# A two-block transformer kernel on one core: own work lists for the last delta rounds, and the stick-breaking softplus of later key blocks added on VectorE

## The reference, cut to what matters

```python
# stick-breaking attention, one head: z[q, k] = q . k / sqrt(128)
visible = key_pos < q_pos
log_keep = where(visible, log_sigmoid(-z), 0)          # -softplus(z)
log_w = log_sigmoid(z) + cumsum_from_the_right(log_keep, keys) - log_keep
o = where(visible, exp(log_w), 0) @ v

# delta rule, one head, chunks in sequence; v is silu(conv(...)) too
u, w = solve(I + lower, [v * beta, k * beta * exp(g)])
v_new = u - w @ S
o = q_dec @ S + attn @ v_new
S = S * g_last + k_dec.T @ v_new
```

## Time and profile before

| | us |
|---|---|
| median of three runs | 2892.74 |
| profiled execution | 2892.34 |
| its span | 2890.1 |
| TensorE busy | 2813.6 (97%) |
| VectorE busy | 1480.2 (51%) |
| ScalarE busy | 1141.9 (40%) |
| GpSimd busy | 513.5 (18%) |
| start of delta round 6 (first fill of unit 41) | 1942.50 |
| first product of the stick stage | 2096.03 |
| first weights product of head 0 | 2133.54 |

### The profile page before, as it was taken

How to read it: one execution, slowest core, us unless ns; L and a number is a source line. 1 busy time by engine, 2 the same in 40 slices (tenths; PEclk the granted TensorE clock), 3 DMA queues, 4 the chain that set the end, 5 groups by cost and what they waited for, 6 DMA issues and landing times.

```text
span 2890.1 us, 37115 instructions
## 1 busy us (share of the span) xinstructions
PE 2813.6 (97%) x14501; PEld 2248.5 (78%) x14501; DVE 1480.2 (51%) x2064; ACT 1141.9 (40%) x1699; POOL 513.5 (18%) x297
## 2 busy tenths in 40 slices
PE   8999999999999999998999999999989999999999
PEld 4888888856656688887888888887867777788887
DVE  6634434266547533336755565554256665653443
ACT  4211212224444422224655555553376553432221
POOL 0000000023111000003434443434322223100000
PEclk9999999999999999999999999999999999999999
DMA  6522323143103233323211121211211113322332
GB/s 233 157 75 89 105 77 103 51 153 97 37 30 142 85 92 92 95 94 103 71 48 49 52 66 54 65 45 45 68 56 52 59 44 104 97 96 94 95 95 80
DMA packets 69872, 241.77 MB, mean 84 GB/s; under 512 B 8219, under 2 KB 8347, under 8 KB 69315
## 3 DMA queue, kind: packets, MB, share of 16 engines
q1 hardware_dynamic: 62032, 221.28, 23.9%
q10 hardware_dynamic: 7666, 18.13, 1.9%
HBM read 232.74 MB, written 6.64 MB: 83 GB/s over the span
## 4 chain that ended last, share of the span: by engine, by line
PE 87%; ACT 6%; DVE 5%; issue 1%; DMA 1%; ACTq 0%; DVEq 0%; POOL 0%; SPq 0%; POOLq 0%
PE ps L1076 61%; PE ps L1460 3%; PE ps L1266 2%; PE ps L1554 2%; PE ps L1235 2%; PE ps L1357 2%; PE ps L1397 2%; PE ps L1253 1%; PE ps L1287 1%; PE ps L1389 1%; ACT w_hi L447 1%; PE ps L1106 1%; PE ps L1531 1%; ACT r L447 1%; DVE f_t L465 1%
## 5 line engine op out<-in xcount | busy, mean ns | idle before, releaser
L1076 PE MATMUL ps<-Nh,w_hi 128*128 128x512 f32 (+1 forms) x1808 | 661.6, 366 | 14.3 <-DVE Nl L454 6.2
L1076 PE MATMUL ps<-Nl,w_hi 128*128 128x512 f32 (+1 forms) x1808 | 630.7, 349 | 0.0
L1076 PE MATMUL ps<-Nh,w_lo 128*128 128x512 f32 (+1 forms) x1808 | 628.4, 348 | 0.0
L447 ACT ACTIVATE w_hi<-w_raw 128x1024 fp32r<-128x1024 f32 (+1 forms) x352 | 368.1, 1046 | 638.4 <-PE ps L1076 524.2
L454 POOL TENSOR_TENSOR w_lo<-w_raw,w_hi 128x1024 fp32r<-128x1024 f32 x125 | 307.7, 2462 | 780.2 <-ACT w_hi L447 776.4
L454 DVE TENSOR_TENSOR w_lo<-w_raw,w_hi 128x1024 fp32r<-128x1024 f32 (+1 forms) x227 | 281.8, 1242 | 257.4 <-ACT w_hi L447 247.3
L1076 PEld LDWEIGHTS ps<-Nh,w_hi 128*128 128x128 f32 x1808 | 343.2, 190 | 85.4 <-issue 35.4
L1076 PEld LDWEIGHTS ps<-Nl,w_hi 128*128 128x128 f32 x1808 | 343.4, 190 | 50.8 <-issue 6.0
L1076 PEld LDWEIGHTS ps<-Nh,w_lo 128*128 128x128 f32 x1808 | 343.2, 190 | 44.0
L1076 PE MATMUL ps<-x1h,w_hi 128*128 128x512 f32 (+1 forms) x784 | 272.3, 347 | 3.3 <-DVE x1l L465 1.9
L1076 PE MATMUL ps<-x1l,w_hi 128*128 128x512 f32 (+1 forms) x784 | 266.6, 340 | 0.0
(11 more groups left out here) (345 smaller groups left out, 4749.5 us busy)
## 6 DMA issues: line engine op xcount, KB each, us to landing
w_raw<-in_w_in SPq DMA_DIRECT2D x132, 512.0 KB, 3.5
w_raw<-in_w_proj SPq DMA_DIRECT2D x89, 512.0 KB, 3.5
w_raw<-in_w_ada SPq DMA_DIRECT2D x52, 512.0 KB, 4.3
w_raw<-in_w_out SPq DMA_DIRECT2D x48, 448.0 KB, 3.3
w_raw<-in_w_out SPq DMA_DIRECT2D x24, 512.0 KB, 3.5
w_raw<-in_w_mix_in SPq DMA_DIRECT2D x19, 512.0 KB, 3.7
w_raw<-in_w_bdn SPq DMA_DIRECT2D x16, 512.0 KB, 3.5
w_raw<-in_w_mix_out SPq DMA_DIRECT2D x8, 512.0 KB, 3.5
```

Of the source, the lines that this page charges most:

```text
L447: self.then_inc(self.e.activation(out, in_, func, **kw), sem)
L1076: ins = e.matmul(out[:, 512 * j:512 * j + n], a[:, kk, :], x[:, kk, c0:c0 + n], start=k == 0 and p == 0, stop=k == nt - 1 and p == 2)
```

## The change

Three tables that give steps their places are replaced or added, `siluv` of head 7 is taken out of round 5 and put into round 6, round 6 begins its branch products one unit later, the factor 0.9 goes, and the stick stage's first part and `p4`/`vt` of every round get other places. In `softplus` VectorE now adds up, in unused columns of the softplus tile, the sums that key blocks 0 and 1 need from the blocks two and more later: `q1` = blocks 2+3+4 for block 1 (columns 384 to 528), `q0` = blocks 1 to 4 at those columns and 1+2 at columns 256 to 384, for block 0. `weights` then uses, for blocks 0 and 1, one product by `tri`, one by `ones` over the 128 columns that only the next block reaches, and one by `ones` over the ready sum.

```diff
-LAST_SCAN = ((0, "v0"), (6.02, "s0"), (6.52, "k1"), (6.52, "v1"), (6.71, "s1"), (10.88, "k2"),
+LAST_SCAN = ((0, "v0"), (4.52, "s0"), (6.52, "k1"), (8.52, "v1"), (8.52, "s1"), (10.88, "k2"),
...
-L2_LAST = ((18.91, "siluz"), ... (26.13, "stq1"), ... (34.48, "stk2"), (42.3, "siluv"))
+L2_LAST = ((18.91, "siluz"), ... (25.13, "stq1"), ... (40.98, "stk2"))
+LATE_PREPARE = ((1.35, "pair"), (6.9, "turn"), (9.6, "x1"), (11.2, "u1"), (17.7, "x2"), ...
+LATE_SCAN = ((7.95, "v0"), (7.95, "siluv"), (7.95, "s0"), (7.95, "k1"), (9.83, "v1"), (12.1, "s1"), ...
...
+        elif i + 2 == NH:
+            fills = products("w_proj", units[0:1]) + beside(units[1], branches[0:4], 2) \
+                + beside(units[2], branches[4:8], 2) + products("w_proj", units[3:])
...
-            steps += [(at, s, i + 1) for at, s in PREPARE]
+            steps += [(at, s, i + 1) for at, s in (PREPARE if i + 2 < NH else LATE_PREPARE)]
...
-            steps += [(at, s, i) for at, s in (SCAN if i + 1 < NH else LAST_SCAN)]
-        if i + 2 == NH:
-            steps = [(at * 0.9, s, h) for at, s, h in steps]
+            steps += [(at, s, i - (s == "siluv")) for at, s in (SCAN if i + 2 < NH else LATE_SCAN if i + 1 < NH else LAST_SCAN)]
...
-          (13.55, "z4"), (13.55, "l4"), (13.55, "p4"), (13.55, "vt"))
+          (13.55, "z4"), (13.55, "l4"), (17.55, "p4"), (17.55, "vt"))
-FIRST_NORMS = ((3, "qsq"), (3, "nq"), (6, "ksq"), (7, "nk"))
-SECOND_NORMS = ((13, "qsq"), (18, "nq"), (25, "ksq"), (30.5, "nk"))
+FIRST_NORMS = ((1.42, "qsq"), (2.85, "nq"), (5.7, "ksq"), (5.7, "nk"))
+SECOND_NORMS = ((13, "qsq"), (18, "nq"), (19, "ksq"), (22.5, "nk"))
-FIRST_SCORES = ((14.3, "z0"), (16.02, "l0"), ... (32.45, "z4"), (32.45, "l4"), (32.45, "p4"), (32.45, "vt"))
+FIRST_SCORES = ((16.3, "z0"), (19.3, "l0"), ... (35.45, "z4"), (35.45, "l4"), (35.45, "p4"), (35.45, "vt"))
...
+    def later(self, h, jb):
+        at, n = ((0, T2 - 2 * P), (T2 - 2 * P, T2 - 3 * P))[jb]
+        return self.SP[h % 2][:, 4, at:at + n]
...
-        w.wait_ge(s.z_sp, 10 * h + 10)
+        w.wait_ge(s.z_sp, 14 * h + (14 if jb < 2 else 12))
...
-        for j2 in range(jb + 1, 5):
-            ins = e.matmul(bank[0:n, j2 * P - c0:wd], cs("ones", SIZES[j2], n), SP[0:SIZES[j2], j2, j2 * P:T2],
-                           start=False, stop=j2 == 4)
+        if jb < 2:
+            mid = (jb + 2) * P
+            e.matmul(bank[0:n, mid - P - c0:mid - c0], cs("ones", P, n), SP[0:P, jb + 1, mid - P:mid],
+                     start=False, stop=False)
+            ins = e.matmul(bank[0:n, mid - c0:wd], cs("ones", P, n), t.later(h, jb), start=False, stop=True)
+        else:
+            for j2 in range(jb + 1, 5):
+                ins = e.matmul(bank[0:n, j2 * P - c0:wd], cs("ones", SIZES[j2], n), SP[0:SIZES[j2], j2, j2 * P:T2],
+                               start=False, stop=j2 == 4)
...
+        SP, q0, q1 = t.SP[h % 2], t.later(h, 0), t.later(h, 1)
+        if jb == 2:
+            w.tt(q0[:, 0:P], SP[:, 1, 2 * P:3 * P], SP[:, 2, 2 * P:3 * P], ALU.add, s.z_sp)
+        elif jb == 3:
+            w.tt(q1, SP[:, 2, 3 * P:T2], SP[:, 3, 3 * P:T2], ALU.add, s.z_sp)
+        elif jb == 4:
+            w.tt(q1[0:n, P:P + n], q1[0:n, P:P + n], d, ALU.add, s.z_sp)
+            w.tt(q0[:, P:], q1, SP[:, 1, 3 * P:T2], ALU.add, s.z_sp)
```

More of the change, by code:

```diff
@@ L71 @@
         (70.5, "parts"), (74.5, "hiz"))
-LAST_SCAN = ((0, "v0"), (6.02, "s0"), (6.52, "k1"), (6.52, "v1"), (6.71, "s1"), (10.88, "k2"),
-             (13.58, "v2"), (17.99, "s2"), (21.23, "k3"), (22.82, "v3"), (23.7, "s3"), (29.7, "k4"),
-             (33.71, "v4"), (36.84, "s4"), (40.32, "nsq"), (42.43, "norm"), (50.14, "gain0"), (50.86, "gain1"),
-             (51.45, "parts"), (51.97, "hiz"))
+LAST_SCAN = ((0, "v0"), (4.52, "s0"), (6.52, "k1"), (8.52, "v1"), (8.52, "s1"), (10.88, "k2"),
+             (13.58, "v2"), (17.99, "s2"), (20.73, "k3"), (22.82, "v3"), (23.7, "s3"), (29.7, "k4"),
+             (33.21, "v4"), (36.34, "s4"), (39.82, "nsq"), (41.93, "norm"), (49.64, "gain0"), (50.36, "gain1"),
+             (50.95, "parts"), (51.47, "hiz"))
 L2NORM = ((19.5, "siluqk"), (21, "siluz"), (23, "l2q"), (23, "lnq"), (27, "stq0"), (27, "stq1"),
@@ L82 @@
             (59.1, "siluv"))
-L2_LAST = ((18.91, "siluz"), (21.38, "siluqk"), (22.99, "l2q"), (22.99, "lnq"), (25.08, "stq0"), (26.13, "stq1"),
-           (27.17, "stq2"), (30.21, "l2k"), (30.21, "lnk"), (30.21, "stk0"), (33.44, "stk1"), (34.48, "stk2"),
-           (42.3, "siluv"))
+L2_LAST = ((18.91, "siluz"), (21.38, "siluqk"), (22.99, "l2q"), (22.99, "lnq"), (25.08, "stq0"), (25.13, "stq1"),
+           (27.17, "stq2"), (30.21, "l2k"), (30.71, "lnk"), (30.71, "stk0"), (33.94, "stk1"), (40.98, "stk2"))
+LATE_PREPARE = ((1.35, "pair"), (6.9, "turn"), (9.6, "x1"), (11.2, "u1"), (17.7, "x2"), (22.2, "u2"),
+                (28.2, "x3"), (32.7, "u3"), (35.7, "x4"), (40.2, "u4"), (46.7, "x5"), (49.7, "u5"),
+                (56.9, "x6"), (60.5, "u6"))
+LATE_SCAN = ((7.95, "v0"), (7.95, "siluv"), (7.95, "s0"), (7.95, "k1"), (9.83, "v1"), (12.1, "s1"),
+             (16.67, "k2"), (19.21, "v2"), (23.63, "s2"), (27.41, "k3"), (28.59, "v3"), (31.72, "s3"),
+             (32.73, "k4"), (39.25, "v4"), (44.52, "s4"), (45.66, "nsq"), (48.43, "norm"), (58.57, "gain0"),
+             (59.51, "gain1"), (59.51, "parts"), (63.7, "hiz"))
 FIRST_HEAD = ((9.9, "siluqk"), (13.95, "l2q"), (14.04, "lnq"), (18, "stq0"), (18.45, "stq1"), (18.45, "stq2"),
@@ L200 @@
           (4.58, "z2"), (4.58, "l2"), (9.62, "p2"), (9.9, "z3"), (10.01, "l3"), (11.28, "p3"),
[L201 removed]
+          (13.55, "z4"), (13.55, "l4"), (17.55, "p4"), (17.55, "vt"))
 BRANCHES = ((0.5, "b0"), (1.5, "b1"), (4, "b2"), (5, "b3"), (6, "b4"), (7.5, "b5"),
             (8.5, "b6"), (10, "b7"))
[L204 to L205 removed]
+FIRST_NORMS = ((1.42, "qsq"), (2.85, "nq"), (5.7, "ksq"), (5.7, "nk"))
+SECOND_NORMS = ((13, "qsq"), (18, "nq"), (19, "ksq"), (22.5, "nk"))
 LAST_BRANCHES = ((6.3, "b0"), (9.9, "b1"), (10.8, "b2"), (11.7, "b3"), (11.7, "b4"), (19.5, "b5"),
                  (19.5, "b6"), (20.4, "b7"))
[L208 to L211 removed]
+THIRD_NORMS = ((9.87, "qsq"), (12.5, "nq"), (19.08, "ksq"), (19.08, "nk"))
+FIRST_SCORES = ((16.3, "z0"), (19.3, "l0"), (22.05, "p0"), (22.1, "z1"), (22.32, "l1"), (24.85, "p1"),
+                (25.4, "z2"), (25.62, "l2"), (30.15, "p2"), (30.7, "z3"), (30.92, "l3"), (33.45, "p3"),
+                (35.45, "z4"), (35.45, "l4"), (35.45, "p4"), (35.45, "vt"))
 NORMS = ((9, "qsq"), (11, "nq"), (17, "ksq"), (19, "nk"))
```

4 lines of the change are left out of this document (removed).

## The result

The changed kernel takes 2868.5 us (median of 4 runs, 2865.5 to 2874.5); the kernel before took 2892.5 beside it (4 runs, 2891.8 to 2896.8). The ratio is 0.9915, 95% interval 0.9903 to 0.9927: 24 us less. Forecast were 2873.5, so 19 less, and the time lies in the range. The profiled execution is one of 2865.5 us, span 2863.3.

What follows compares the result with a forecast made beforehand. TensorE, busy 97% of the span, was taken as the bound. Terms 12.3 + 1.5 + 2.5 + 0.8 + 1.9 + 1.2 = 20.2, less 1.2, left 19.0 off 2892.3; forecast 2873.5 us, range 2869 to 2877 (chance 0.60).

Steps and rivals of the forecast that it cites:

- products saved: Stick rounds, weights of key blocks 1 and 0: fewer products save 0.54 and 1.00 us a head, 12.3 us for eight heads.
- p4 and vt later: Stick rounds: TensorE's 0.36 us wait at the key norm for ScalarE's square goes in five rounds; 1.5 us taken, bounds 0 and 2.
- first scores: Start of the stick stage: head 1's key norm moves ahead of softplus, first weights start earlier; 2.5 us gained.
- round 6 (0.8 and 1.9): Delta round 6: 0.8 us gained at the round's start, 1.9 us from the vanished wait for Z's bank.
- round 7: Delta round 7: a branch product and a fill between the scan steps remove two of three TensorE waits, 1.2 us.
- new small waits: Rounds with less TensorE work to cover waits, VectorE at 76%: 1.2 us given back from the sum.
- Cost taken: 0: Stick rounds: VectorE's four additions, about 1.1 us a round, stay covered by six fills, except for head 0; cost 0.
- A: Rival: only the saved products count, new places win nothing as each wait is replaced; 2880 us; chance 0.19 together with E.
- B: Rival: stick-round additions meeting GpSimd's low part delay VectorE and reach TensorE, 1.4 us a round, 11 in all; 2884.5; chance 0.08.
- C: Rival: slower, TensorE waits at hand-overs behind `turn` in round 6 and falls to half clock; 2901.7 us; 0.04 with milder forms.
- D: Rival: more slack than seen, weights start at 2130, round 6 has no wait behind `turn`; 2867 us; chance 0.09.
- E: Rival: 0.32 us is a group's opening price and stays, columns alone count, 8.1 us saved; 2877.7; chance 0.19 with A.

## Why the prediction was nearly right

By its terms, in us (forecast, then measured in the traces from the start of round 6 on; by the medians the change is worth 24.0):

```
products saved          12.3   15.8   (8 x 1.98)
p4 and vt later          1.5    2.4   (5 x 0.48)
first scores             2.5    2.0   (2.6 by the places, 0.6 back for the additions)
round 6 (0.8 and 1.9)    2.7    1.5
round 7                  1.2    1.8
clock in round 7         0      1.7   (not forecast)
new small waits         -1.2   -0.7   (what is left to the sum)
sum                     19.0   24.5
```

**Products.** The step that failed is "block 1 ... which saves 0.54. Block 0 ... saves 1.00": the prices in the chain were right to 0.02 us, but the price of a 16-row product was read from its own group only. It also costs 0.19 and 0.21 in the groups behind, and that makes 3.2 of the 5 us by which the forecast missed. It could have been read from the trace of before: of the branch groups of a round, all of three equal products, the one in the earlier trace rows took 0.70 and those behind a group by `ones` 0.89 to 0.91. The bounds I gave, 8.1 to 12.3, did not hold the value, since both took a piece of the chain to end where its row ends.

**Additions.** "Cost taken: 0" held in the full rounds (2.47 us a round won, with the additions once and twice) and failed by 0.6 for head 0, where nothing stands between: first scores 2.6 without and 2.0 with them. The cover was sized by the wrong thing. I gave the six fills behind `p4`, 4.2 us, to the weights, the low part and the key norm alike. The key norm is the tight one, and its cover is the 3.2 us that VectorE has ahead of it: with four times the additions the waits stand there, and none at the weights of later rounds. VectorE's share of busy time came out at 74% (24.40 of 33 us, 76% forecast).

**Key norm.** Right in its cause (five waits of 0.36 go, and come back with `p4` and `vt`), low by 0.12 a round, which no wait in the trace explains. The last line of the table is no reading of waits but a remainder; it lies in the last two stick rounds, which win 0.5 and 0.2 less than the others by the products alone.

**First scores, rounds 6 and 7.** The new waits came where and as long as forecast: 4.9 at `pair` (4.8), none for Z's bank, 5.3 at the first weights on VectorE. The first weights stand 35.5 us behind the first product of the stick stage, 37.5 before: 2.0 and not 2.5, 0.6 of it for the additions. Round 7 won half as much again as forecast by its steps. Round 6 won 1.5 where 2.7 was forecast: with the 1.9 for Z's bank gone, the rest of it did not win 0.8 but lost 0.4. Waits of 4.9, 0.9, 0.6 and 0.5 stand there in place of 6.7 and 0.3. The 1.7 of clock in round 7 made up for that: no term of the forecast has it, so that part of the nearness is luck. In the sum itself, 2873.3 and 0.4 make 2873.7 and not 2873.5.

**The rivals.** A (only the products) falls: the places alone win 9.5 [0.9945 to 0.9972]. B's mechanism is real: a meeting costs 2.0 to 2.2 on VectorE, as priced, and where meetings use up the slack, waits and clock make it dearer. But its condition is not met in the changed kernel. C did not come: no wait in round 6 behind `turn` is over 0.9. D gave 2867 and is by the number the nearest, for the wrong reason: it took the products at their price and put the rest into waits. E falls by the kernel without 16-row products.

## What to carry over

Read a product's price as the time from the start of its group to where the next group of the same work runs at its usual length; a small product may charge its neighbour. On an engine that isn't the bound, slack is what stands idle ahead of the one step that the bound waits for, not its share of busy time: 74% busy meant 3.2 us here. Beyond it the added work also moves everything behind it into new meetings, and the clock falls in the waits: 2.7 us of additions a round cost 49 us in all here. Where tiles have a short tail, try to fill it with zeros once and use whole tiles: with this kernel it won 1.2% to before where the change alone won 0.85%, though not at every product (w4 won nothing).
